# Sixteen experts in straight-line code, a choice of tokens in two half lists, and a last expert that is placed by a matmul before the final norm

## What is computed

```python
aff = softmax(h @ w_router)                      # h: (1024, 1024), 16 experts
g, idx = top_k(aff.T, 128)                       # each expert takes its best 128 tokens
y_e = (silu(h[idx] @ w_gate[e]) * (h[idx] @ w_up[e])) @ w_down[e]    # width 2816 inside
x = x + g2 * zeros.at[idx].add(g * y_e)          # summed over the experts
out = x * rsqrt(mean(x * x) + 1e-6) * final_g
```

## Time and profile before

| | us |
|---|---|
| median of three runs (3159.37 to 3164.81) | 3161.08 |
| the profiled execution, its own time | 3166.16 |
| its span in the profile | 3164.4 |
| PE busy | 2822.7 (89%) |
| DVE busy | 2192.4 (69%) |
| ACT busy | 1552.2 (49%) |
| POOL busy | 71.1 (2%) |

### The profile page before, as it was taken

One profiled execution on the slowest core, in us unless ns is written; L12 is line 12 of the kernel. 1 busy time (PEld: TensorE's weight loads), 2 busy tenths in 40 slices (PEclk: granted clock), 3 DMA queues, 4 the chain that ended last, 5 costly groups with the idle time before them and its releaser, 6 DMA issues. The chain is left out here.

```text
span 3164.4 us, 37561 instructions
## 1 busy us (share of the span) xinstructions
PE 2822.7 (89%) x13251; PEld 2237.1 (71%) x13251; DVE 2192.4 (69%) x2113; ACT 1552.2 (49%) x1579; POOL 71.1 (2%) x37
## 2 busy tenths in 40 slices
PE   6899999788888884988199999999999999999994
PEld 2788888688644442767088887887878878788784
DVE  4340010466469999554888888898888888888884
ACT  4221122465421110222177776776767767677673
POOL 0000000000000000000000000000000000000000
PEclk8899999898999997998599999999999999999997
DMA  5222122532112121443299999999999999999994
GB/s 206 69 98 89 57 80 73 104 63 44 40 47 77 64 78 45 149 158 121 95 388 383 384 374 362 371 386 354 379 352 370 375 358 376 359 360 380 361 376 178
DMA packets 168181, 710.64 MB, mean 225 GB/s; under 512 B 28952, under 2 KB 66048, under 8 KB 100402
## 3 DMA queue, kind: packets, MB, share of 16 engines
q1 hardware_dynamic: 163300, 691.46, 58.4%
q0 software_dynamic: 4752, 17.30, 2.1%
HBM read 668.05 MB, written 40.67 MB: 224 GB/s over the span
## 5 line engine op out<-in xcount | busy, mean ns | idle before, releaser
L1868 DVE TENSOR_TENSOR moe_w_lo<-raw,moe_w_hi 128x2048 fp32r<-128x2048 f32 x528 | 1208.0, 2291 | 197.1 <-ACT moe_w_hi L1820 196.8
L1820 ACT ACTIVATE moe_w_hi<-raw 128x2048 fp32r<-128x2048 f32 x528 | 1012.6, 1919 | 382.9 <-PE moe_ps_gate L1786 165.1
L1786 PE MATMUL moe_ps_gate<-moe_w_hi,moe_xt_hi 128*128 128x512 f32 (+1 forms) x768 | 294.9, 384 | 26.2 <-issue 16.8
L1786 PE MATMUL moe_ps_up<-moe_w_hi,moe_xt_hi 128*128 128x512 f32 (+1 forms) x768 | 293.1, 382 | 0.0
L1786 PE MATMUL moe_ps_gate<-moe_w_hi,moe_xt_lo 128*128 128x512 f32 (+1 forms) x768 | 291.0, 379 | 0.0
L1786 PE MATMUL moe_ps_gate<-moe_w_lo,moe_xt_hi 128*128 128x512 f32 (+1 forms) x768 | 290.4, 378 | 0.0
L1786 PE MATMUL moe_ps_up<-moe_w_hi,moe_xt_lo 128*128 128x512 f32 (+1 forms) x768 | 286.6, 373 | 0.0
L1786 PE MATMUL moe_ps_up<-moe_w_lo,moe_xt_hi 128*128 128x512 f32 (+1 forms) x768 | 286.1, 373 | 0.0
L560 DVE TENSOR_TENSOR proj_w_lo<-w_in,proj_w_hi 128x2048 fp32r<-128x2048 f32 x20 | 45.7, 2290 | 275.6 <-ACT proj_w_hi L472 275.6
L1776 PE MATMUL moe_ps_y<-moe_w_hi,moe_ht_hi 128*128 128x512 f32 x704 | 218.6, 392 | 0.0
L1776 PE MATMUL moe_ps_y<-moe_w_lo,moe_ht_hi 128*128 128x512 f32 x704 | 217.0, 389 | 0.0
(11 more groups left out here) (243 smaller groups left out, 4323.2 us busy)
## 6 DMA issues: line engine op xcount, KB each, us to landing
raw<-in_w_moe SPq DMA_DIRECT2D x528, 1024.0 KB, 5.9
w_in<-in_w_in SPq DMA_DIRECT2D x20, 1024.0 KB, 5.7
hyena_w_mod<-in_w_mod SPq DMA_DIRECT2D x16, 1024.0 KB, 5.3
norm_w_mod<-in_w_mod SPq DMA_DIRECT2D x4, 2048.0 KB, 14.6
g_d<-proj_stage SPq DMA_DIRECT2D x16, 512.0 KB, 2.6
merge_gate<-g_d SPq DMA_DIRECT2D x16, 512.0 KB, 4.5
u_d<-proj_conv SPq DMA_DIRECT2D x12, 512.0 KB, 2.8
attn_k_raw<-qk_d SPq DMA_DIRECT2D x16, 320.0 KB, 6.0
```

Source lines behind the costliest of these rows:

```text
L1786: mm = pe.matmul(ps, hp[:, s, k, :], wp[:, r, :], start=(k == 0 and x == 0), stop=(k == KD - 1 and x == 2))
L1820: act.activation(w_hi[:, n % PARTS], raw[:, n % RAW], ACT.Copy).then_inc(hi_ready, 1)
L1868: dve.tensor_tensor(w_lo[:, n % PARTS], raw[:, n % RAW], w_hi[:, n % PARTS].bitcast(F32), ALU.subtract).then_inc(lo_ready, 1)
```

## The change

It has three parts.

1. **The choice in two halves.** The tokens are split in two halves of 512. The rows are now 32 (expert and half) x 512, turned by four transposes of 32 columns. The 16 rounds stay. Each half gives its own sorted 128 best; the second list is mirrored (two further copies), four transposes bring both lists and their positions back, and a few small operations take, place by place, the larger of the first list's value and the mirrored second's, with its position.
2. **The experts written out.** No loops: all 16 experts stand in the queues one after the other. The ring `raw` has 8 slots. The next expert's tokens are turned at the last down units of chunks 2 and 3, units 21 and 27. POOL issues a gather once the tokens before it have been turned, and waits for a scatter's landing only ahead of the next scatter. The unused seventeenth gather and its transposes are gone.
3. **The last expert and the norm.** The final norm is moved into the experts' block. SP loads the sums `acc_d` (without the last expert's rows) into the first four slots of `raw` as the last weight units leave them. For the last expert DVE builds a 0/1 matrix `pick` (which row goes to which token, one 128 x 128 block per tile of tokens), forms `y` in two halves, and splits each in high and low part with ACT; PE multiplies `pick` with both for each tile (four matmuls) into `ps_gate` and `ps_up` in turn, and DVE adds the sum to the tile. Squares, inverse root, scaling and stores follow in the same block. ACT takes a square root of ones ahead of it.

```diff
-RAW = 6
+RAW = 8
...
+                for j in range(TT // 2):
+                    mm = pe.transpose(ps_r[0:2 * E_N, j * P:(j + 1) * P], halves[:, j, :], ident[:])
                 mm.then_inc(aff_turned, 1)
+                pe.wait_ge(best_ready, 3)
+                for x, src in enumerate((best[:], mirror[:, 0, :], where_f[:], mirror[:, 1, :])):
+                    mm = pe.transpose(ps_c[:, x, :], src, ident[0:2 * E_N, 0:2 * E_N])
+                mm.then_inc(best_turned, 1)
...
+                dve.tensor_tensor(halves[:].rearrange("p j (g e) -> p g j e", g=2),
+                                  aff[:].rearrange("p (g j) e -> p g j e", g=2),
+                                  wide(inv).rearrange("p (g j) e -> p g j e", g=2), ALU.mult).then_inc(aff_ready, 1)
                 dve.wait_ge(aff_turned, 1)
-                dt.then_wait(dve.tensor_copy(rows[:], ps_r[0:E_N, :]))
+                dt.then_wait(dve.tensor_copy(rows[:], ps_r[0:2 * E_N, :]))
...
+                dve.tensor_copy(mirror[:, 0, :], best[:, ::-1]).then_inc(best_ready, 1)
+                dve.tensor_copy(mirror[:, 1, :], where[:, ::-1]).then_inc(best_ready, 1)
                 dve.wait_ge(best_turned, 1)
+                dt.then_wait(dve.tensor_copy(lists[:], ps_c[:]))
+                first, second = (lists[:, x, x * E_N:(x + 1) * E_N] for x in (0, 1))
+                at_first, at_second = (lists[:, 2 + x, x * E_N:(x + 1) * E_N] for x in (0, 1))
+                dt.inc(dve.tensor_tensor(ahead[:], first, second, ALU.is_ge))
+                dt.inc(dve.scalar_tensor_tensor(out=gap[:], in0=at_second, scalar=float(T // 2), in1=at_first,
+                                                op0=ALU.add, op1=ALU.subtract))
+                dve.tensor_tensor(gate_col[:], first, second, ALU.max)
+                dt.wait()
+                dt.then_wait(dve.tensor_tensor(gap[:], gap[:], ahead[:], ALU.mult))
+                dve.scalar_tensor_tensor(out=idx_col[:], in0=at_second, scalar=float(T // 2), in1=gap[:],
+                                         op0=ALU.add, op1=ALU.subtract)
...
+        FREE = N_ALL - PARTS
+        assert N_ALL % RAW == 0
+        x = raw[:, 0:TT // 2].rearrange("p s (t d) -> p (s t) d", d=D)
+        pick = w_hi[:, FREE % PARTS, 0:D].rearrange("p (t q) -> p t q", q=P)
+        y_hi, y_lo = w_hi[:, FREE % PARTS, D:2 * D], w_lo[:, FREE % PARTS, 0:D]
+        gain, squares = sl[:].rearrange("p a b -> p (a b)"), xe
+        ps_sum = [t[:].rearrange("p a b -> p (a b)") for t in (ps_gate, ps_up)]
...
-        TURN_X = {0: LAST_OF["down", 0], 1: LAST_OF["down", 1]}
+        TURN_X = {0: LAST_OF["down", 2], 1: LAST_OF["down", 3]}
...
-                with sp.Fori(0, PAIRS_E - 1) as i:
-                    for n in range(RAW, 2 * N_U):
-                        load(i, n)
-                    for n in range(RAW):
+                sp.dma_start(spot[:], a["spot"]).then_inc(spot_in, 16)
+                for g in range(RAW, N_ALL):
+                    sp.wait_ge(lo_ready, g - RAW + 1)
+                    sp.dma_start(raw[:, g % RAW], unit_source(a, g // N_U, g % N_U)).then_inc(raw_in[g % RAW], 16)
+                acc, dst = a["acc_d"].rearrange("(t p) d -> p t d", p=P), out[0].rearrange("(t p) d -> t p d", p=P)
+                sp.wait_ge(scattered, 16 * (E_N - 1))
+                for t in range(0, TT, 2):
+                    sp.wait_ge(lo_ready, N_ALL - RAW + t // 2 + 1)
+                    sp.dma_start(x[:, t:t + 2], acc[:, t:t + 2]).then_inc(acc_in[t // GROUP], 16)
+                sp.wait_ge(multiplied, N_C * E_N)
+                sp.dma_start(gain, bass.AP(a["final_g"].tensor, 0, [[0, P], [1, D]])).then_inc(gain_in, 16)
+                for t in range(TT):
+                    sp.wait_ge(out_ready, t + 1)
+                    sp.dma_start(dst[t], x[:, t]).then_inc(out_stored, 16)
+                sp.wait_ge(out_stored, 16 * TT)
...
                 gather(0)
                 for e in range(E_N):
-                    gather(e + 1)
+                    if e + 1 < E_N:
+                        pool.wait_ge(turned_x, 2 * e + 2)
+                        gather(e + 1)
+                    if e == E_N - 1:
+                        break
                     pool.wait_ge(y_ready, e + 1)
+                    if e:
+                        pool.wait_ge(scattered, 16 * e)
                     pool.indirect_dma_start(acc, bass.IndirectOffsetOnAxis(ap=idx_col[:, e:e + 1], axis=0), y[:], None,
                                             compute_op=ALU.add).then_inc(scattered, 16)
-                    pool.wait_ge(scattered, 16 * e + 16)
-                    pool.sem_inc(y_free, 1)
+                pool.wait_ge(scattered, 16 * (E_N - 1))
...
-                            if TURN_X[half] == u:
+                            if TURN_X[half] == u and e + 1 < E_N:
                                 turn_x(e + 1, half)
-                for s in range(2):
-                    expert(s, s)
-                with pe.Fori(1, PAIRS_E) as i:
-                    for s in range(2):
-                        expert(2 * i + s, s)
+                for t in range(TT):
+                    pe.wait_ge(picked, 1)
+                    if t >= 2:
+                        pe.wait_ge(added, t - 1)
+                    for n in range(2):
+                        cols = slice(n * 512, (n + 1) * 512)
+                        pe.wait_ge(y_high, n + 1)
+                        pe.matmul(ps_sum[t % 2][:, cols], pick[:, t, :], y_hi[:, cols], start=True, stop=False)
+                        pe.wait_ge(y_low, n + 1)
+                        mm = pe.matmul(ps_sum[t % 2][:, cols], pick[:, t, :], y_lo[:, cols], start=False, stop=True)
+                    mm.then_inc(placed, 1)
 
...
+                act.wait_ge(step, 1)
+                act.activation(root[:], var[:], ACT.Sqrt)
+                act.wait_ge(used, FREE + 1)
+                for n in range(2):
+                    act.wait_ge(y_half, n + 1)
+                    cols = slice(n * 512, (n + 1) * 512)
+                    act.activation(y_hi[:, cols], y[:, cols], ACT.Copy).then_inc(y_high, 1)
+                for t in range(TT):
+                    act.wait_ge(added, t + 1)
+                    if t:
+                        act.wait_ge(squared, t)
+                    act.activation(squares[:], x[:, t], ACT.Square, accum_out=ss[:, t:t + 1]).then_inc(squared, 1)
+                    if t % GROUP == GROUP - 1:
+                        tiles = slice(t + 1 - GROUP, t + 1)
+                        act.wait_ge(var_ready, t // GROUP + 1)
+                        act.activation(root[:, tiles], var[:, tiles], ACT.Sqrt).then_inc(rooted, 1)
...
+                dt = Tally(dve, step)
+                dt.then_wait(dve.memset(var[:], 1.0))
+                dt.then_wait(dve.tensor_copy(token[:], idx_col[:, E_N - 1:E_N]))
+                dve.wait_ge(spot_in, 16)
+                dt.then_wait(dve.tensor_scalar(chosen[:], spot[:, P:P + TT], -1.0, token[:], ALU.mult, ALU.add))
...
+                        elif what == "y" and e == E_N - 1:
+                            dve.wait_ge(used, FREE + 1)
+                            dve.tensor_tensor(pick, spot[:, 0:P].unsqueeze(1).broadcast_to([P, TT, P]),
+                                              chosen[:].unsqueeze(2).broadcast_to([P, TT, P]), ALU.is_equal
+                                              ).then_inc(picked, 1)
+                            dve.wait_ge(used, N_ALL)
+                            dve.wait_ge(scattered, 16 * e)
+                            for n in range(2):
+                                cols = slice(n * 512, (n + 1) * 512)
+                                dve.scalar_tensor_tensor(out=y[:, cols], in0=ps_y[:, cols], scalar=gate_col[:, e:e + 1],
+                                                         in1=g2_row[:, cols], op0=ALU.mult, op1=ALU.mult
+                                                         ).then_inc(y_half, 1)
+                            for n in range(2):
+                                cols = slice(n * 512, (n + 1) * 512)
+                                dve.wait_ge(y_high, n + 1)
+                                dve.tensor_tensor(y_lo[:, cols], y[:, cols], y_hi[:, cols].bitcast(F32), ALU.subtract
+                                                  ).then_inc(y_low, 1)
...
+                def add(t):
+                    dve.wait_ge(acc_in[t // GROUP], 16 * GROUP // 2)
+                    dve.wait_ge(placed, t + 1)
+                    dve.tensor_tensor(x[:, t], ps_sum[t % 2], x[:, t], ALU.add).then_inc(added, 1)
...
-                        dve.scalar_tensor_tensor(out=o[:, t], in0=x[:, t], scalar=inv[:, t:t + 1], in1=gain[:],
+                        dve.scalar_tensor_tensor(out=x[:, t], in0=x[:, t], scalar=inv[:, t:t + 1], in1=gain,
                                                  op0=ALU.mult, op1=ALU.mult).then_inc(out_ready, 1)
...
+                for t in range(GROUP + 1):
+                    add(t)
+                variance(0)
```

(77 more changed lines are left out.)

171 lines of the change are left out of this document (44 added, 127 removed).

## The result

The changed kernel takes 3087.8 us (median of four runs, 3085.2 to 3091.9), the kernel before beside it 3162.9 us (four runs, 3159.4 to 3171.8). The ratio is 0.9759, with a 95% interval of 0.9736 to 0.9783: faster by 75 us or 2.4%. The forecast of 3089.6 us is 1.8 us off. The forecast saving of 71.5 us is 3.7 us short; the two differ because the kernel before has a median of 3162.9 us here and of 3161.1 in the runs that the forecast started from.

A forecast was written before the change was run, and what follows sets the result against it. The prediction took the experts to be bound by PE, with DMA just keeping up. Savings of 25.1 (choice), 35.4 (experts) and 11.0 (end) sum to 71.5 us: from a median of 3161.1 to 3089.6 us, range 3075 to 3110.

The forecast's parts named there:

- The choice: Choice ahead of the experts: 47 searches at half the columns, less the added merge steps, save 25.1 us.
- The rival in which searches don't get shorter: In the choice, two lists each cost as much as one: 25.2 + 0.5 us go missing, 3115 us; chance 0.04.
- Jumps and gathers: Experts: written-out code removes six loop jumps, the moved gather its four stalls; together 42.2 us saved.
- The moved turning: Experts: ACT's new step delays a chain PE waits for by 0.5 us in 15 experts, 7.5 us given back.
- The sign named for it: Profile after: 0.8 us of idle weight loads ahead of turning the last chunk's `h`, in place of 0.31.
- The end: From the last expert's `y` to the end: scatter, meeting and load go, placing and adds come; 11.0 us saved.
- The 0.6 us taken for the clock: At the end, a few tiles' four matmuls at PE's low clock take 0.4 us more than an add: 0.6 us.
- Loads as the bound: Experts: without jumps DMA cannot catch up, an expert needs about 98 us, time 3154 us; chance 0.07.
- Fetching the code: Experts: long straight code runs dry; one 5.58 us stop per expert gives 3179 us, slower; chance 0.03.
- The end at the low clock: Placing at the end: all eight tiles slow, 3.2 us, part saves 8.4, time 3092 us; chance 0.05.
- the main case: Whole kernel: forecast without the rivals, 3075 to 3105 us including 3 us for differing runs; chance 0.81.

The follow-up runs named there:

- the earlier place: Changed kernel with the next expert's tokens turned one down unit earlier, at units 15 and 21: 3084.1 us, ratio 0.9742; again 3084.8 us, ratio 0.9745.
- the doubled steps: Changed kernel with ACT's split, or in another kernel DVE's step, for the second half of the next tokens made twice: 3103.2 and 3091.5 us, single times.

## Why the prediction was right, term by term

**The choice: 25.1 forecast, 24.8 measured.** The step that carried it, that a search halves like an elementwise operation (537 ns less), held: 534, 531 and 532 ns less. In proportion to the columns it would have been 605. The rival in which searches don't get shorter is out.

**Jumps and gathers: 42.2 forecast.** With the turning out of the way the interval is 93.74 us in all experts, against the 93.78 taken. The sum was right, but it does not divide into a price for each edit: the gathers' share is 7 us with the loops in place and 14 to 21 without, so each edit's worth depends on whether the other is in. Where the prediction says of the moved gather that its four stalls go, the profiled run with the old order in straight code has seven. With the loops written out and the old order kept, only some 21 to 28 of the 42.2 us would have come.

**The moved turning: 7.5 forecast, 6.4 measured** (0.43 x 15, between the changed kernel's 94.17 and the 93.74 of the earlier place). The cause was named rightly, ACT's step and not DVE's; the doubled steps show it. The price was 0.43 to 0.48 us for a step of 0.58 to 0.60; ACT's next step starts 0.48 us behind the start of this one (1635.92 and 1636.40), so the overlap of its steps is the difference. The sign named for it, 0.8 us of idle weight loads in place of 0.31, came as 10.7 / 15 = 0.71 on average. What the prediction did not ask is whether the move was needed. It was not. With 42.2 + 0.7 - 6.4 = 36.5 the experts' 37.1 us is met to 0.6.

**The end: 11.0 forecast, 11.8 measured.** The first add begins 3.46 us behind `y` (forecast 3.4), the eight adds with what stands between end at 3071.99, 10.24 later (forecast 10.3). The 0.6 us taken for the clock was not paid. Windows of the changed kernel at the end, two early and two late microseconds of the placing (columns as in the earlier trace rows):

```profile
3060.00:3062.00 2.00, 1.84 (x7) 1.09 (x8) 1.34 (x3) 0.37 (x1) 0.00 (x0) 1.00 0.00 0
...
3068.00:3070.00 2.00, 1.69 (x6) 1.16 (x7) 1.83 (x4) 1.62 (x4) 0.00 (x0) 1.00 0.00 0
```

PE had been idle 1.66 us, then worked in bursts, and the granted clock stayed at 1.00, its level of 2.4 GHz. The repeated fall that the Trainium skill describes (TensorE: Matmul & The Clock Gate, "A second HAM failure mode: psum-queue depth-cycling") did not come about here: the part saved 11.8 us, near the 11.0 that went by the rows and not the 8.4 that went by the Trainium skill's rule.

**The rivals.** *Loads as the bound*: the interval is 94.18 us, not 98, and ACT never waits for `raw`, though a unit's median landing went from 5.9 to 7.1 us; six slots do as well. *Fetching the code*: with 34727 instructions in straight queues PE has no idle time put down to issue between 1600 and 3040 us, where the loops had 16.8 us of it. *The end at the low clock*: above.

One slip of the range: with the price of the moved turning at 19, the choice at 25.1 and the end at 8.4, the main case's upper end is 3103.7, and 3 more is 3107, not 3105. It changes nothing here.

Some of the closeness is luck: the profiled executions differ by 3.4 us in a stretch that no edit touches, and two medians of the changed kernel by 2.7 (3087.8 and 3090.5).

What stays open: how the 4 to 8 us of a jump divide between PE's own restart and the other engines', why a stall for a gather can be longer in straight code, and the wide spread of the kernel with the choice alone.

## What to carry to other kernels

Price an edit against the stalls that remain when the other edits are in: a wait can be hidden by one that you are about to remove, so measure such parts in pairs. Where a step is put into another engine's queue, follow the chain behind that place to the bounding engine: 0.6 us on an engine that is idle half the time cost 0.43 to 0.48, a longer step on the engine beside it not at all. And when a transfer comes too late, first move its issue; moving its use as well can cost more than it brings.

## What was unexpected of the hardware

- PE's wait for a gather can cost more than its length. The 3.05 us stall was followed by a granted clock of 0.50 for some 3 us, and that interval (marks at 1791.33 and 1889.79) was 98.46 us, 4.72 over the straight one: 1.67 more than the stall. The seven stalls fall into two kinds: those of 1.92, 2.00, 2.89 and 3.05 us were followed by a granted clock of 0.50 to 0.77 and cost 1.7 to 1.8 us beyond their length, those of 0.41, 1.61 and 1.67 us left it at 1.00 and cost 0.2 beyond it. The 1.66 us of idle time at the end left the clock at 1.00 too.
- A searching operation of DVE got cheaper with half the columns on twice the partitions: 32 partitions x 512 took 664 to 682 ns, 16 x 1024 took 1196 to 1216.
- A unit's landing got 1.2 us longer, and nothing waited for it. Neither the jumps nor the ring account for most of it: with the gathers' old order it is 5.9 us in the loops and 6.0 in straight code with eight slots, with the new order and the late turning 6.6 in the loops, 7.1 in straight code and 7.2 there with six slots, with the new order and the turning at units 9 and 15 it is 6.5. So it goes in the main with the gathers' order and the place of the turning; the cause is not shown.
